# Split rows of the experts in blocks of 128 columns: one layout change in a trunk layer on one Trainium2 core

## What is computed

```python
def expert_choice_ffn(h, w_router, w_gate, w_up, w_down):
    B, n, D = h.shape
    cap = EC_FACTOR * n // N_EXPERTS
    aff = jax.nn.softmax((h @ w_router).astype(jnp.float32), axis=-1)
    vals, idx = lax.top_k(aff.swapaxes(1, 2), cap)
    xs = jax.vmap(lambda hb, ib: hb[ib])(h, idx)
    hid = jax.nn.silu(jnp.einsum('becd,edf->becf', xs, w_gate)) * jnp.einsum('becd,edf->becf', xs, w_up)
    ye = jnp.einsum('becf,efd->becd', hid, w_down) * vals[..., None].astype(h.dtype)
    return jax.vmap(lambda ib, yb: jnp.zeros((n, D), yb.dtype).at[ib.reshape(-1)].add(yb.reshape(-1, D)))(idx, ye)
```

## Time and profile before

| | |
|---|---|
| median of three runs | 2908.04 us (2907.46 to 2911.56) |
| profiled execution | 2914.9 us, span 2913.3 us |
| TensorE busy in the span | 2802.4 us (96%) |
| VectorE, ScalarE, GpSimd busy | 2130.9, 1505.5, 287.8 us |
| expert stage, 1775 to 2871 us | TensorE busy 1095.15 of 1096 us |
| granted TensorE clock, mean | 0.984 of full |

### The profile page before, as it was taken

How to read it: one execution, slowest core, us unless ns; L and a number is a source line. 1 busy time by engine, 2 the same in 40 slices (tenths; PEclk the granted TensorE clock), 3 DMA queues, 4 the chain that set the end, 5 groups by cost and what they waited for, 6 DMA issues and landing times.

```text
span 2913.3 us, 42799 instructions
## 1 busy us (share of the span) xinstructions
PE 2802.4 (96%) x15868; PEld 2281.8 (78%) x15868; DVE 2130.9 (73%) x1909; ACT 1505.5 (52%) x1468; POOL 287.8 (10%) x342
## 2 busy tenths in 40 slices
PE   7999999999999999999999986999999999999994
PEld 4689999999999999999988874666666666666662
DVE  2349678696777777763353677888888888888886
ACT  4411221215555555552242454777777777777774
POOL 1000000002111111100000001111011111011000
PEclk9999999999999999999999997999999999999997
DMA  9978668674333333364443756999999999999996
GB/s 334 332 250 268 212 196 278 212 246 141 121 120 118 118 118 117 97 211 123 125 139 130 289 202 264 363 392 391 390 388 390 389 384 384 380 389 390 381 400 230
DMA packets 301277, 757.87 MB, mean 260 GB/s; under 512 B 20344, under 2 KB 184736, under 8 KB 236528
## 3 DMA queue, kind: packets, MB, share of 16 engines
q1 hardware_dynamic: 275376, 639.52, 60.3%
q0 software_dynamic: 23264, 101.24, 10.7%
q10 hardware_dynamic: 2544, 15.82, 1.3%
HBM read 700.61 MB, written 55.89 MB: 260 GB/s over the span
## 4 chain that ended last, share of the span: by engine, by line
PE 89%; DVE 5%; DMA 2%; issue 2%; ACT 1%; SPq 0%; DVEq 0%; ACTq 0%; POOLq 0%
PE ps L496 16%; PE ps L497 16%; PE ps L498 16%; PE ps L2223 9%; PE ps L2224 9%; PE ps L2225 9%; PE ps L2354 3%; PE ps L2356 2%; PE ps L2355 2%; PE ps L2080 2%; PE ps L2292 1%; DVE mod_acc L1471 1%; DVE rsd L1697 1%; DMA raw<-in_w_mod 1%; PE ps L2103 1%
## 5 line engine op out<-in xcount | busy, mean ns | idle before, releaser
L430 DVE TENSOR_TENSOR we_lo<-raw,we_hi 128x2048 fp32r<-128x2048 f32 x384 | 876.4, 2290 | 127.8 <-ACT we_hi L425 126.7
L425 ACT ACTIVATE we_hi<-raw 128x2048 fp32r<-128x2048 f32 x384 | 736.8, 1919 | 275.7 <-PE ps L498 275.7
L2223 PE MATMUL ps<-hi,w_lo 128*128 128x320 f32 x2048 | 643.1, 314 | 3.3 <-DVE w_lo L401 2.5
L2224 PE MATMUL ps<-lo,w_hi 128*128 128x320 f32 x2048 | 633.6, 309 | 4.5 <-issue 4.5
L2225 PE MATMUL ps<-hi,w_hi 128*128 128x320 f32 x2048 | 633.4, 309 | 0.0
L401 DVE TENSOR_TENSOR w_lo<-raw,w_hi 128x2048 fp32r<-128x2048 f32 (+1 forms) x123 | 272.9, 2221 | 198.2 <-ACT w_hi L391 180.3
L497 PE MATMUL ps<-we_lo,xs_hi 128*80 128x512 f32 x1024 | 403.2, 394 | 0.0
L496 PE MATMUL ps<-we_hi,xs_lo 128*80 128x512 f32 x1024 | 402.5, 393 | 0.1
L498 PE MATMUL ps<-we_hi,xs_hi 128*80 128x512 f32 x1024 | 400.4, 391 | 0.0
L2223 PEld LDWEIGHTS ps<-hi,w_lo 128*128 128x128 f32 x2048 | 385.2, 188 | 13.3 <-issue 10.6
L2224 PEld LDWEIGHTS ps<-lo,w_hi 128*128 128x128 f32 x2048 | 385.4, 188 | 5.1 <-issue 5.0
(11 more groups left out here) (397 smaller groups left out, 3773.7 us busy)
## 6 DMA issues: line engine op xcount, KB each, us to landing
raw<-in_w_e_gate SPq DMA_DIRECT2D x128, 1024.0 KB, 7.2
raw<-in_w_e_up SPq DMA_DIRECT2D x128, 1024.0 KB, 7.2
raw<-in_w_e_down SPq DMA_DIRECT2D x128, 1024.0 KB, 11.7
raw<-in_w_in SPq DMA_DIRECT2D x144, 512.0 KB, 5.3
mod_raw<-in_w_mod SPq DMA_DIRECT2D x64, 1024.0 KB, 5.3
raw<-in_w_mod SPq DMA_DIRECT2D x64, 512.0 KB, 7.0
raw<-in_w_o SPq DMA_DIRECT2D x64, 512.0 KB, 4.9
d_proj<-stage POOLq DMA_DIRECT2D x32, 320.0 KB, 3.3
```

Of the source, the lines that this page charges most:

```text
L425: act.activation(we_hi[:, k % NEH, :], raw_slot(k), ACT.Copy).then_inc(hi_ready, 2)
L430: TTn(we_lo[:, k % NEH, :], raw_slot(k), we_hi[:, k % NEH, :].bitcast(F32), ALU.subtract).then_inc(lo_ready, 2)
L2223: pe.matmul(out, wl, hi[:, k, ms], start=(k % 16 == 0), stop=False)
L2224: pe.matmul(out, wh, lo[:, k, ms], start=False, stop=False)
```

## The change

The four arrays get blocks of 128 columns (512 bytes) instead of 80 (320 bytes), of which columns 0 to 79 are used. `xs_hi` stays where it is, `xs_lo` starts 8192 bytes behind it, `hid_hi` another 8192 bytes on, and `hid_lo`, for which there is no more room there, moves behind the last raw buffer. The stationary operands are still 80 columns wide. The operations that fill the arrays write 6 or 4 pieces of 80 elements (and VectorE's read `xs_hi` and `hid_hi` in such pieces) where they wrote one row of 480 or 320; what they read from PSUM stays packed. `by_block` is a new helper that only views a row as pieces. At the start of the program, `xT` is written from PSUM in four pieces of 128 elements that lie 640 apart (line 933 on ScalarE, line 1358 on VectorE), though the profile gives its form as 128x512; `v_stage` (line 1401) and `pT_hi` (line 1073) are written as one row of 512. No instruction is added, removed or moved on any engine by the change; line numbers behind 415 shift.

```diff
--- before.py
+++ after.py
@@ -273,12 +273,12 @@
         we_lo = at("we_lo", [P, NEH, D], F32R, split_at + NEH * UB)
         eb = split_at + 2 * NEH * UB
         E = place(eb, [("xs", [P, D], F32), ("ye", [P, D], F32), ("hid", [P, D_EXP], F32)])
-        xs_hi = at("xs_hi", [P, KT, CAP], F32R, eb + 20480)
-        xs_lo = at("xs_lo", [P, KT, CAP], F32R, eb + 20480 + 5120)
-        hid_hi = at("hid_hi", [P, 8, CAP], F32R, eb + 20480 + 10240)
-        hid_lo = at("hid_lo", [P, 8, CAP], F32R, eb + 20480 + 12800)
+        xs_hi = at("xs_hi", [P, KT, P], F32R, eb + 20480)
+        xs_lo = at("xs_lo", [P, KT, P], F32R, eb + 20480 + KT * P * 4)
+        hid_hi = at("hid_hi", [P, 8, P], F32R, eb + 20480 + 2 * KT * P * 4)
+        hid_lo = at("hid_lo", [P, 8, P], F32R, late + UB + 192)
         raw2_at = rb + 2 * UB
-        assert eb + 35840 <= raw2_at
+        assert eb + 20480 + 2 * KT * P * 4 + 8 * P * 4 <= raw2_at and (late + UB + 192 - eb) % (P * 4) == 0
         raw2 = at("raw2", [P, 3, D], F32, raw2_at)
         assert raw2_at + 3 * UB <= rb + KT * N_TOK * 4
         raw3 = at("raw3", [P, D], F32, late)
@@ -413,6 +413,10 @@
         def exp_loads(e, k):
 
             return (Q_EXP * INC if k % NSLOT < NRAW else 0) + (UNITS // NSLOT * e + k // NSLOT + 1) * 16
+
+        def by_block(x):
+
+            return x.rearrange("p (k n) -> p k n", n=CAP)
 
         def exp_unit(e, k):
             return Q_EXP * NRAW + e * UNITS + k
@@ -1263,8 +1267,7 @@
             def take_xs(e, par):
                 for g, ks in enumerate(XS_GROUPS):
                     act.wait_ge(S["xsT_done"], 3 * e + g + 1)
-                    act.activation(xs_hi[:, ks, :].rearrange("p k n -> p (k n)"),
-                                   ps[:, 4 * par + 1 + g, 0:(ks.stop - ks.start) * CAP], ACT.Copy).then_inc(S["xs_hi_done"], 1)
+                    act.activation(xs_hi[:, ks, 0:CAP], by_block(ps[:, 4 * par + 1 + g, 0:(ks.stop - ks.start) * CAP]), ACT.Copy).then_inc(S["xs_hi_done"], 1)
 
             def expert(e, par, last):
                 a_, b_ = 4 * par, 4 - 4 * par
@@ -1280,8 +1283,7 @@
                     if k == 17:
                         for h in range(2):
                             act.wait_ge(S["hidT_done"], 2 * e + h + 1)
-                            act.activation(hid_hi[:, 4 * h:4 * h + 4, :].rearrange("p k n -> p (k n)"),
-                                           ps[:, (a_, b_)[h], 0:4 * CAP], ACT.Copy).then_inc(S["hidT_hi"], 1)
+                            act.activation(hid_hi[:, 4 * h:4 * h + 4, 0:CAP], by_block(ps[:, (a_, b_)[h], 0:4 * CAP]), ACT.Copy).then_inc(S["hidT_hi"], 1)
                     if k == 19 and not last:
                         take_xs(e + 1, 1 - par)
                 act.wait_ge(halves_used, used(exp_unit(e, UNITS)))
@@ -1993,8 +1995,8 @@
             def take_xs(e, par):
                 for g, ks in enumerate(XS_GROUPS):
                     dve.wait_ge(S["xs_hi_done"], 3 * e + g + 1)
-                    hi_, lo_ = (x[:, ks, :].rearrange("p k n -> p (k n)") for x in (xs_hi, xs_lo))
-                    TTn(lo_, ps[:, 4 * par + 1 + g, 0:(ks.stop - ks.start) * CAP], hi_.bitcast(F32), ALU.subtract
+                    TTn(xs_lo[:, ks, 0:CAP], by_block(ps[:, 4 * par + 1 + g, 0:(ks.stop - ks.start) * CAP]),
+                        xs_hi[:, ks, 0:CAP].bitcast(F32), ALU.subtract
                         ).then_inc(S["xs_lo_done"], 1)
 
             def expert(e, par, last):
@@ -2015,8 +2017,8 @@
                             TTn(hid, hid, ps[0:CAP, a_ + 2 + h, :], ALU.mult).then_inc(S["hid_done"], 1)
                         for h in range(2):
                             dve.wait_ge(S["hidT_hi"], 2 * e + h + 1)
-                            TTn(hid_lo[:, 4 * h:4 * h + 4, :].rearrange("p k n -> p (k n)"), ps[:, (a_, b_)[h], 0:4 * CAP],
-                                hid_hi[:, 4 * h:4 * h + 4, :].rearrange("p k n -> p (k n)").bitcast(F32), ALU.subtract
+                            TTn(hid_lo[:, 4 * h:4 * h + 4, 0:CAP], by_block(ps[:, (a_, b_)[h], 0:4 * CAP]),
+                                hid_hi[:, 4 * h:4 * h + 4, 0:CAP].bitcast(F32), ALU.subtract
                                 ).then_inc(S["hidT_lo"], 1)
                     if k < UNITS:
                         exp_split_lo(dve, e, k)
@@ -2535,7 +2537,7 @@
                         kt = k % 8 * 2 + p
                         if k < 8 and kt % 6 == 0:
                             pe.wait_ge(S["xs_lo_done"], 3 * e + kt // 6 + 1)
-                        expert_half(e, k, p, out, a_ + 2 * (k // 8), xs_hi[:, kt, :], xs_lo[:, kt, :], kt == 0, kt == KT - 1,
+                        expert_half(e, k, p, out, a_ + 2 * (k // 8), xs_hi[:, kt, 0:CAP], xs_lo[:, kt, 0:CAP], kt == 0, kt == KT - 1,
                                     S["up_half"] if k == KT - 1 and p == 1 else None)
                 if not last_one:
                     pe.wait_ge(S["gathered"], (e + 1) * 16 + 16)
@@ -2556,7 +2558,7 @@
                     if k in (0, 4):
                         pe.wait_ge(S["hidT_lo"], 2 * e + k // 4 + 1)
                     for p in range(2):
-                        expert_half(e, KT + k, p, out, a_ + 2 * p, hid_hi[:, k, :], hid_lo[:, k, :], k == 0, k == 7)
+                        expert_half(e, KT + k, p, out, a_ + 2 * p, hid_hi[:, k, 0:CAP], hid_lo[:, k, 0:CAP], k == 0, k == 7)
 
             pe.wait_ge(S["gathered"], 16)
             for ks in XS_GROUPS:
```

## The result

| | before | changed |
|---|---|---|
| median of six runs each | 2910.98 us | 2927.52 us |
| profiled execution's span | 2913.3 us | 2926.9 us |
| expert stage, first to last matmul start | 1775.73 to 2870.64, 1094.9 us | 1776.02 to 2884.26, 1108.2 us |

The changed kernel is slower: ratio 1.0053, 95% interval 1.0042 to 1.0063, which is 12 to 18 us. The medians differ by 16.5 us; the prediction was +15.7, from the 2908.04 us of the first three runs to 2923.7. Of the 13.6 us between the two spans, 13.3 us lie in the expert stage, which also starts 0.3 us later.

A forecast was written before the change was run, and what follows sets the result against it. The prediction took TensorE's matmul start rate to bound the expert stage; 11.7 + 5.2 - 1.2 + 0 = +15.7 us on the earlier median of 2908.04 gave 2923.7 us, range 2907 to 2930 (forecast's own 2918 to 2930).

The forecast's parts named there:

- Step 1: Token tiles of the expert stage: matmul starts go from 229.5 to 233.3 ns apart, over 3072 matmuls, +11.7 us.
- Steps 2 and 3: Inner tiles: 229.9 to 233.3 ns, +5.2 us; TensorE's shorter wait before inner tile 4 gives back 1.2 us.
- Step 4: ScalarE's and VectorE's split writes in pieces of 80 elements: no added cost, 0 with 0 to 5 ns as bounds.
- B: Rival: whole blocks bring the projection's 227.1 ns to the expert stage, gaining 11.7 us, 2896 us; chance 0.10.
- C: Rival: tile place is of no account, the period-four pattern in the expert stage stays, 2908 us; chance 0.10.
- D: Rival: high and low tile loads disturb the expert stream more, 240 ns between starts, 48 us, 2956 us; chance 0.06.

The follow-up runs named there:

- e4: Changed kernel, but loads and matmuls take whole 128-column blocks, columns 80 to 127 zeros: 226.7 ns between starts, expert stage 1085.5 us.
- e1: Changed kernel with tiles in the last 80 columns (48 to 127) of each block: 226.7 or 231.1 ns, stage 1097.4 us, ratio to before 1.0008.
- e6: Changed kernel with 96 columns loaded and multiplied from each block's start: 230.0 ns between starts, expert stage 1097.1 us.
- e5: Changed kernel with the moving operand streamed from 64 bytes later, only time read: 226.7 ns or slower, expert stage 1092.6 us.
- e8: Changed kernel with whole 128-column blocks loaded, run again and timed: ratio to the kernel before 0.9985 (0.9973 to 0.9997), expert stage 1085.2 us.
- e12: Changed kernel with the 80 columns at 32 to 111 of each block, timed: ratio to the kernel before 0.9991 (0.9980 to 1.0002), stage 1088.8 us.
- e7: Changed kernel with 96 columns loaded from column 32 to each block's end: 231.7 ns between starts, expert stage 1103.7 us.
- e11: Changed kernel with only the high tiles (xs_hi, hid_hi) at columns 32 to 111: 228.9 ns over the token part, stage 1091.8 us.

## Why the prediction was right

**What bounds the stage.** TensorE's rate: the stage grew by 13.3 us and the span by 13.6, with VectorE and ScalarE unchanged. The reading holds for a slower TensorE; for a faster one the wait for VectorE before inner tile 4 grows (e4).

**The place modulo 256.** The step that carried everything was reading the mean of 229.5 ns as four values, and taking the dear one for all. It came out to the tenth of a nanosecond. It was in part luck that the change leads to this place: it has one steady rate, while a forecast for the place of tile 3, made in the same way for e1, failed, as that place has two. Counting both start and end as the same class kept the prediction safe from a question it couldn't answer; e4 and e6 show that the end matters and the start doesn't set the rate alone, and e5 that the moving operand has a part in it.

**Step 1, token tiles, +11.7 us.** An expert's token part grew by what was forecast, 3.8 ns on 192 matmuls. Only the first expert did not. Its first matmuls ran at half the clock, and that lasted shorter this time: the granted clock was 0.50, the lower level of 1.2 GHz, from 1776.0 to 1778.3 us here and from 1775.7 to 1780.5 before. Ahead of them TensorE had mostly waited since the projection: it was busy for 10.7 of 45 us before and for 11.6 of 46 here. In the changed kernel:

```profile
1776.02 0.71 PE L500 MATMUL ps<-we_hi,xs_lo 128*80 128x512 f32 x1
...
1778.23 0.54 PE L502 MATMUL ps<-we_hi,xs_hi 128*80 128x512 f32 x1
1778.61 0.40 PE L500 MATMUL ps<-we_hi,xs_lo 128*80 128x512 f32 x1
```

Up to the sixth start five distances at half rate, some 0.43 us each, and durations of 0.63 us instead of 0.40. The kernel before, first and twelfth start:

```profile
1775.73 0.71 PE L496 MATMUL ps<-we_hi,xs_lo 128*80 128x512 f32 x1
...
1780.51 0.50 PE L498 MATMUL ps<-we_hi,xs_hi 128*80 128x512 f32 x1
```

Eleven distances in 4.78 us. Six more times 0.2 us is 1.2 us that has nothing to do with the change. This is most of what the profile shows less than forecast, 13.6 against 15.7. It is chance, and it hid nothing: no step of the sum had it.

**Steps 2 and 3, inner tiles, +5.2 - 1.2 us.** The cadence was right. (16 x 0.08 is 1.3, so the sum as worked out is 15.6.) More was given back than forecast: from the last matmul ahead of tile 4 to the second of tile 4 it was 0.60 us and is 2181.53 - 2181.04 = 0.49. That is 0.11 us an expert, 1.8 us in all, where I had 0.08 and 1.2. The whole part grew by 0.19 us in most experts, some 3 us where the two steps make 4.

**Step 4, split writes, 0.** Right. The groups of the changed kernel give six token tiles 650 and 559 ns, against 651 and 560, and the inner high tiles 0.44 us:

```profile
L1998 DVE TENSOR_TENSOR xs_lo<-ps,xs_hi 128x480 fp32r<-128x480 f32 x32 | 19.6, 650 | 2.9 <-ACT xs_hi L1270 2.8
L1270 ACT ACTIVATE xs_hi<-ps 128x480 fp32r<-128x480 f32 x32 | 16.3, 559 | 21.2 <-PE ps L2082 21.2
```

**From the span to the time.** The prediction carried over the 7 us by which the profiled execution before lay above the median. That didn't hold: the changed kernel's profiled execution is 2928.5 us, 1 us above its median of 2927.52. So the span came out 2 us under the forecast of 2929.0 and the median 4 us over 2923.7, and that +15.7 is so near the 16.5 us of the medians is partly luck; the interval is 12 to 18 us.

**The rivals.** B (blocks are clean in themselves) had a true observation under a wrong cause: the projection's 227.1 ns belongs to tiles that fill their block, so that their ends lie at 0. e4 brings that rate to the experts by loading the 48 unused columns too. C fell with tiles 1 to 3. It rested on the rule of the Trainium skill, "TensorE: Matmul & The Clock Gate", section "Step-by-step: what each phase is for", that the weight load has a read port of its own and takes nothing from the running matmul. These runs disagree in so far as the distance between matmuls does depend on where the loaded tile lies, by up to 6.6 ns in 226.7; in what the load and the stream meet, no run shows. The same section's rule that a load's time goes with its columns agrees in the direction, not in proportion: the loads of e4 take 188 ns for 128 columns where 80 take 148. Both are shorter than the distance between two matmuls. D needed a class above 233.3, and no run has one.

## What to carry to other kernels

Read a stream of matmuls from start to start and split the mean by the stationary tile before calling it TensorE's rate: 4 ns of 230 looked like noise and were an address, worth half a per cent of this kernel. For a stream like this one (fp32r, 512 moving columns), look at where each stationary tile ends against the moving operand's start, modulo 256 bytes. Rounding the block up and using its first columns put every tile at the dearest of the places tried. Loading the whole block gave 226.7 ns and the one timed gain clear of noise, 1 to 8 us (e8); the 80 columns at 32 to 111 gave a steady 228.3 and a timed gain that can't be told from none (e12). Letting 80 columns end just at the moving operand's start is no safe choice: it has a slower cadence too, and with it e1's stage came out 2.5 us longer than the packed one. Other formats and other widths of the moving operand weren't tried.

## What was not expected

One layout can have two steady rates. With the tile's end at the moving operand's start, 80-column tiles ran at 226.7 ns in one part and at 231.1 ns in another of the same execution (e1), and changed between them within a part as well, in the places where the program makes TensorE wait and near inner tile 1. In the kernel before I had read packed token tile 3 as 226.7; the single distances of inner tile 3 show the slower sequence (232, 230, 236, 229, 224, 235 ns), those of inner tile 7, at the same place, the fast one. Tiles of 128 columns took the fast cadence in the experts of both profiled executions that have them (e4, e8), apart from some matmuls after the same places, and tiles of 96 columns never did (e7). What sets the choice, and why unlike places of high and low tile don't give the mean (e11), no run here tells.
